# Attention scores: the row maximum of each unit taken in three parts instead of two

## The reference, cut to what matters

```python
s = (jnp.einsum('bqhd,bkhd->bhqk', qn_b, k_nope)
     + jnp.einsum('bqhr,bkr->bhqk', qr_b, k_rope)) * ATTN_SCALE
p = jax.nn.softmax(s.astype(jnp.float32), axis=-1).astype(v.dtype)
return jnp.einsum('bhqk,bkhd->bqhd', p, v)
```

## Time and profile before

| | us |
|---|---|
| median of 3 runs | 1441.85 |
| lowest, highest | 1437.81, 1442.49 |
| the profiled execution | 1438.47 |
| its span | 1436.7 |
| attention in it | 173.5 to 493 |
| PE busy, share of the span | 96% |
| DVE, ACT, POOL busy | 55%, 49%, 31% |

### The profile page before, as it was taken

One profiled execution on the slowest core, in us unless ns is written; L12 is line 12 of the kernel. 1 busy time (PEld: TensorE's weight loads), 2 busy tenths in 40 slices (PEclk: granted clock), 3 DMA queues, 4 the chain that ended last, 5 costly groups with the idle time before them and its releaser, 6 DMA issues.

```text
span 1436.7 us, 20514 instructions
## 1 busy us (share of the span) xinstructions
PE 1373.9 (96%) x7548; PEld 1232.2 (86%) x7548; DVE 797.0 (55%) x1192; ACT 700.9 (49%) x1409; POOL 442.7 (31%) x542
## 2 busy tenths in 40 slices
PE   7898989999999989999999999999999999999996
PEld 2798878999888868899998888999999889999995
DVE  4587577877777754345564456544445555434434
ACT  4777578777767643233333453433334433333332
POOL 3576638787778545350000002100000030000002
PEclk9999999999999999999999999999999999999999
DMA  9421101111111160164444332433333334333321
GB/s 342 132 91 62 28 20 42 43 43 39 42 38 38 51 221 0 45 240 155 146 146 161 117 118 96 182 122 140 117 120 128 130 106 175 117 128 135 117 88 44
DMA packets 50493, 154.63 MB, mean 108 GB/s; under 512 B 9848, under 2 KB 12440, under 8 KB 50424
## 3 DMA queue, kind: packets, MB, share of 16 engines
q1 hardware_dynamic: 49560, 150.60, 29.6%
q0 software_dynamic: 864, 3.15, 0.5%
HBM read 148.73 MB, written 4.83 MB: 107 GB/s over the span
## 4 chain that ended last, share of the span: by engine, by line
PE 62%; DVE 1%; POOL 1%; DMA 0%; ACT 0%; issue 0%; DVEq 0%; POOLq 0%
PE bank L2054 27%; PE bank L2062 27%; PE bank L1776 6%; PE bank L1540 1%; DVE wol L1733 0%; DMA add<-in_w_o 0%; POOL x L1846 0%; DVE w1l L1952 0%; PE bank L2076 0%; DVE sq L1959 0%; DVE rTl L1963 0%; ACT woh L1702 0%; POOL stat L1850 0%; DVE aTl L1726 0%; POOL stat L1869 0%
## 5 line engine op out<-in xcount | busy, mean ns | idle before, releaser
L2054 PE MATMUL bank<-h2h,w1l 128*128 128x384 f32 x768 | 258.4, 336 | 0.0
L2054 PE MATMUL bank<-h2l,w1h 128*128 128x384 f32 x768 | 258.3, 336 | 0.0
L2054 PE MATMUL bank<-h2h,w1h 128*128 128x384 f32 x768 | 258.2, 336 | 0.0
L1846 POOL TENSOR_TENSOR x<-x,xn 128x512 f32<-128x512 f32 x12 | 15.6, 1326 | 713.3 <-DVE xn L1993 713.3
L1952 DVE TENSOR_TENSOR w2l<-w2raw,w2h 128x1024 fp32r<-128x1024 f32 x95 | 116.5, 1226 | 177.3 <-ACT w2h L1883 177.3
L1883 ACT ACTIVATE w2h<-w2raw 128x1024 fp32r<-128x1024 f32 x95 | 100.8, 1061 | 195.9 <-PE bank L2062 195.9
L2062 PE MATMUL bank<-w2h,rTh 128*128 128x512 f32 x576 | 182.8, 398 | 3.7 <-DVE rTl L1963 3.7
L1890 ACT ACTIVATE relu<-bank 128x384 f32<-128x384 f32 x94 | 46.1, 491 | 286.0 <-PE bank L2054 286.0
L2062 PE MATMUL bank<-w2l,rTh 128*128 128x512 f32 x576 | 179.8, 393 | 0.0
L2062 PE MATMUL bank<-w2h,rTl 128*128 128x512 f32 x576 | 178.8, 391 | 0.0
L1959 DVE TENSOR_TENSOR sq<-relu 128x384 f32<-128x384 f32 x96 | 55.6, 579 | 181.3 <-ACT relu L1890 176.4
(11 more groups left out here) (275 smaller groups left out, 2782.2 us busy)
## 6 DMA issues: line engine op xcount, KB each, us to landing
w1raw<-in_w SPq DMA_DIRECT2D x96, 512.0 KB, 3.7
w2raw<-in_w SPq DMA_DIRECT2D x96, 512.0 KB, 4.5
ada_raw<-in_w_ada SPq DMA_DIRECT2D x24, 512.0 KB, 5.5
xn<-in_w_ada SPq DMA_DIRECT2D x16, 512.0 KB, 3.7
xin<-in_x SPq DMA_DIRECT2D x9, 512.0 KB, 4.0
x<-in_x SPq DMA_DIRECT2D x3, 1536.0 KB, 12.4
g_raw<-in_w_ada SPq DMA_DIRECT2D x8, 512.0 KB, 3.5
out_y<-x POOLq DMA_DIRECT2D x6, 512.0 KB, 5.5
```

What stands on the lines that cost most here:

```text
L1846: nc.gpsimd.tensor_tensor(k.x[:, t, cut], k.x[:, t, cut], gated_half(t, i), ALU.add).then_inc(out_added, 1)
L2054: op = nc.tensor.matmul(bank[6 + s][:, 0:BN], w[0][s][x][:, c * P:(c + 1) * P], k.h2[b % 2][y_][:, c, :], start=n == 0, stop=n == 3 * DC - 1)
```

## The change

The maximum is taken in three reduces of 384 columns, one behind each group of scores, so `s_filled` now goes up behind every group. The first two results are joined and scaled while the third is still to come (into a fourth column of `mx`), and a last instruction multiplies the third by -SCALE and takes the smaller of both, which is `nm`. The result is the same number. Per unit DVE issues five instructions instead of three, and waits twice on its own semaphore instead of once. The other engines' instructions are the same; only the counts that they wait for differ.

```diff
-        mx, nm, rs, psum = sb("mx", [P, 4, 2]), sb("nm", [P, 4]), sb("rs", [P, 8]), sb("psum", [P, 8, 2])
+        mx, nm, rs, psum = sb("mx", [P, 4, 4]), sb("nm", [P, 4]), sb("rs", [P, 8]), sb("psum", [P, 8, 2])
...
-                    act.wait_ge(nm_ready, 3 * u + 3)
+                    act.wait_ge(nm_ready, 5 * u + 5)
...
-                    for part, (lo, hi) in enumerate(((0, 2), (2, 3))):
-                        dve.wait_ge(s_filled, 2 * u + part + 1)
-                        nc.vector.tensor_reduce(mx[:, s, part:part + 1], scores_in[:, lo:hi, :], AX_XY, ALU.max).then_inc(nm_ready, 1)
-                    dve.wait_ge(nm_ready, 3 * u + 2)
-                    nc.vector.tensor_scalar(nm[:, s:s + 1], mx[:, s, 0:1], mx[:, s, 1:2], -SCALE, ALU.max, ALU.mult).then_inc(nm_ready, 1)
+                    for c in range(3):
+                        dve.wait_ge(s_filled, 3 * u + c + 1)
+                        nc.vector.tensor_reduce(mx[:, s, c:c + 1], scores_in[:, c:c + 1, :], AX_XY, ALU.max).then_inc(nm_ready, 1)
+                        if c == 1:
+                            dve.wait_ge(nm_ready, 5 * u + 2)
+                            nc.vector.tensor_scalar(mx[:, s, 3:4], mx[:, s, 0:1], mx[:, s, 1:2], -SCALE, ALU.max, ALU.mult).then_inc(nm_ready, 1)
+                    dve.wait_ge(nm_ready, 5 * u + 4)
+                    nc.vector.scalar_tensor_tensor(nm[:, s:s + 1], mx[:, s, 2:3], -SCALE, mx[:, s, 3:4], ALU.mult, ALU.min).then_inc(nm_ready, 1)
...
-                        if c:
-                            op.then_inc(s_filled, 1)
+                        op.then_inc(s_filled, 1)
```

## The result

The changed kernel takes 1450.15 us (median of 5 runs, 1447.73 to 1451.18), the kernel before 1441.85 (1436.81 to 1443.36). The ratio of all runs is 1.0065, with a 95% interval of 1.0047 to 1.0083: 0.65%, or 9.4 us, slower (the two medians alone are 8.3 us apart). The forecast was 1449 us.

A forecast was written before the change was run, and what follows sets the result against it. No single engine is full; attention is a ring of scores, maximum, exponent and next scores. Longer DVE queue 4.9 us plus GpSimd holds 4 us make 9 us on 1440, forecast 1449 us, range 1441 to 1459.

The forecast's parts named there:

- The sum: Whole kernel: 4.9 us of longer DVE queue plus 4 us of holds, 9 us on a base of 1440.
- What one maximum costs on DVE: Attention, DVE behind: three reduces, join and last instruction take 1.93 us against 1.67, 0.26 longer.
- Where the early one doesn't count: 36 free units: `nm` comes 0.19 us earlier, but ScalarE is still busy with `phi`, so nothing is gained.
- Where the late one counts: Units t = 3, 4: two longer maxima delay `kTl` by 0.52 us in seven heads; with smaller parts, 4.9 us.
- 3 x 0.26 for ScalarE's other waits: Three units outside the counted chains where ScalarE waits for `nm`: each passes on 0.26, 0.8 us in all.
- The last instruction's second operand: Last instruction, two SBUF tensors: waits for GpSimd's running two-operand instruction in some 22 units; 4 us, between 0 and 9.6.
- The discount of 0.15: Last instruction of the maximum: a hold costs the rest of GpSimd's running instruction less about 0.15 us.
- the units t = 1 and 5 have 0.5 of room and swallow it: Units t = 1 and 5: 0.5 us of room before ScalarE's exponent absorbs a hold, so they cost nothing.
- The page's wording: DVE/GpSimd shared port: `krT` would hold two-SBUF-input instructions too, second term about half as large again; forecast followed the trace.
- longer queue, but no hold: Rival: the one-element last instruction slips in beside GpSimd, only the 4.9 us queue term counts; 1445, chance 0.24.
- heavier: Rival: holds pile up from unit to unit, or `krT` holds too; 9 + 9 us, 1458, chance 0.10.
- The signs that I had named: Attention about 328 us, closing stage unchanged; `kTl` wait about 6, `nm` wait 8 or more; free units' exponents no earlier.

The follow-up runs named there:

- e3: Kernel before, with three reduces only in units t = 1, 2, 5, 6 (pointer-scalar last instruction), two elsewhere; ratio 1.0003 to the kernel before.
- e1: Changed kernel with the last instruction taking the joined value as pointer scalar instead of a second SBUF tensor; ratio 1.0046 to the kernel before.
- e4: Kernel before, with three reduces only in units t = 3 and 4 (pointer-scalar last instruction), two elsewhere; ratio 1.0016 to the kernel before.
- e7: Changed kernel with a last instruction that only scales the third part by a constant, ignoring the joined value; ratio 1.0018 to the kernel before.
- e9: Kernel before with `attn` moved to the next unit's end and three reduces everywhere, pointer-scalar last instruction; ratio 1.0003 to the kernel before.
- e2: Kernel before, two reduces, with the join multiplying by a one-column SBUF tensor instead of a constant; ratio 1.0040 to the kernel before.
- e8: Kernel before with only `attn` moved from the end of unit t = 3 or 7 to the next unit's end; ratio 1.0006.

## Why the prediction was right

- **The sum**: 9 us forecast, 9.4 measured. Two terms, both in the right direction, but with sizes off in opposite senses (4.9 forecast and 2.6 measured, 4 forecast and 5.8 to 6.8 measured): the agreement to half a microsecond is luck, the sign and the order of size aren't.
- **What one maximum costs on DVE**: right. The reduces are 547 ns at the median (545 assumed), the last instruction 160 (160). From the first of the two reduces at 246.96 to the end of the last instruction, without its hold, it is 1.92 (1.93 forecast).
- **"Where the early one doesn't count"**: right, shown by the free unit and by e3.
- **"Where the late one counts", first term 4.9 us**: the mechanism is right (the t = 3 and 4 units of e1, e4 and e7, and e9), the term was mis-sized. It measured 2.6 us in time (0.9 to 4.5) and 3.4 in the stretch. I charged 0.52 in seven heads and 0.5 in the last. In e7 four of the seven and the last paid that; the third had only one maximum in the chain, the fourth a hold of `attn` that took some of it, the sixth waited elsewhere. Of the 3 x 0.26 for ScalarE's other waits two came (0.26 and 0.25 in the units 39 and 47), and unit 40 took 0.26 less.
- **"The last instruction's second operand", second term 4 us**: the mechanism is right (e2, and e7 against the changed kernel), the term was mis-sized the other way: 1.0065 against 1.0018 is 6.8 us, e2 gives 5.8. How often was good: 19 and 26 above 260 ns in two kernels, 22 forecast (of the 19, 16 beside the kinds that I had counted, 2 beside other two-tensor instructions, 1 beside `krT`); 11.1 and 12.8 us of DVE time, 9.6 forecast. The discount of 0.15 was right: the held instruction ends 0.02 behind GpSimd's and takes 0.16 anyway, so that it loses the rest of GpSimd's less 0.14. What went wrong is how much gets through. The step "the units t = 1 and 5 have 0.5 of room and swallow it" held for holds of that size and the exponent alone: the units 57 and 61 of the changed kernel were held for 0.50 and 0.55 and took no longer (0.00 and 0.02). It forgot that a `kTl` stands behind the maximum of t = 1: the units 25 and 33, held for 0.50 and 0.41, took 0.37 and 0.28 longer. And it took the mean of 0.44 for every hold; one of 1.1 passes any room, in a unit of any t.
- **The page's wording** (the Trainium skill, "SBUF — State Buffer", sections "SBUF: two separate sides" and "Who interferes with whom"): two-operand GpSimd instructions hold the DVE instruction to their end, as the page says. For `krT`, one tensor operand, the prediction's reading was too short. By the page's wording it would hold for its whole 1.57 us; it holds for the first 0.70. The `attn` at 240.90, on which the prediction rests, started 0.72 behind `krT`'s start at 240.18, just outside. So did the last instruction at 243.99, which took 0.16 in this one:

```profile
243.07 3.12 POOL L617 TENSOR_SCALAR krT<-xn,sf 128x512 f32<-128x512 f32 x2
```

  In the changed kernel `krT` gave one of the 19 long ones (0.40) and one of 0.22, so that the sum lost little by it.
- **The rival "longer queue, but no hold"** (1445) falls by the 1253 ns. The "heavier" one, with holds that pile up, had a chance of 0.10; some of it is in the 0.95 of PE's wait at 378.09, but the total stayed under it.
- **The signs that I had named**: ScalarE's wait for `nm` 12.5 (8 or more forecast), PE's for `kTl` 5.1 (about 6), the free unit's exponent unmoved. The stretch grew by 9.4, the closing stage didn't.

## What to carry to other kernels

Cutting a reduction in parts so that it starts earlier pays only where its engine waits for the data and its reader waits for it; look at both waits, unit by unit, since here half of the units had the first and almost none the second. Where the engine is behind, what is added to such a step is paid in full, once per such step in a chain that somebody waits for, unless another wait in the chain takes it up. And on VectorE beside a busy GpSimd, take the second operand of a small instruction as a pointer scalar, not as a second SBUF tensor, above all in front of an instruction that another engine waits for.

## What the runs showed of the hardware that I had not expected

- A VectorE instruction of one element per partition with two SBUF tensor inputs can last 1253 ns instead of 158, if GpSimd has just started a two-tensor instruction. It ends 0.013 to 0.023 us behind GpSimd's. The same computation with a pointer scalar took 212 to 215 ns in 64 of 64 cases.
- Beside GpSimd's product of a 128x512 tensor with a pointer scalar (1.57 us) such an instruction is held too, but only until 0.70 us behind GpSimd's start: 9 of 9 that started 0.16 to 0.48 behind it, none of 26 that started later.
- The pointer scalar costs 54 to 60 ns more than a constant (214 against 154 to 160), and in this kernel even that showed: e1 against e7 is 1.0046 against 1.0018, 4.0 us with some 2.6 of uncertainty, and 2.3 us in the stretch, 1.1 of them at the lower clock. How much of its 3.5 us of DVE time was paid stays open.
- The stage ahead of attention takes between 173.3 and 176.5 us in executions of kernels that don't differ there; the 3.1 us are a third of the effect under study.
- A wait of TensorE can be followed by a second cost: in e8 PE waited 1.78 us, the granted clock was 0.76 over the unit behind it, and this unit took 6.12 instead of 5.17 without waiting for anything.
